# A two-block hybrid layer stack in split fp32: the feed-forwards' high weight parts get homes of their own, and the arena begins later

## The reference

```python
# first block
x = x + mix @ w_out                                   # mix: causal pools and an RWKV-7 scan
h2 = rms_norm(x, mlp_norm)
x = x + square(relu(h2 @ w_ffn_up)) @ w_ffn_down      # 2048 -> 8192 -> 2048
gate = sigmoid(rms_norm(x, ple_norm) @ w_ple_gate)    # 2048 -> 2048
x = x + gate * (p @ w_ple_proj)
x = rms_norm(x, final_norm)
# second block
h = x + concat([gla_out, nsa_out]) @ w_out_2          # gated linear attention, sparse attention
m = rms_norm(h, ffn_norm_g_2)
return h + (silu(m @ w_gate_2) * (m @ w_up_2)) @ w_down_2   # 2048 -> 5632 -> 2048
```

## Time and profile before

| | us |
|---|---|
| median of 3 runs | 2490.66 |
| lowest and highest | 2487.08, 2492.56 |
| the profiled execution's own time | 2493.05 |
| its span, first to last instruction | 2491.2 |
| mean granted TensorE clock | 0.993 |

### The profile page before, as it was taken

How to read it: one execution, slowest core, us unless ns; L and a number is a source line. 1 busy time by engine, 2 the same in 40 slices (tenths; PEclk the granted TensorE clock), 3 DMA queues, 4 the chain that set the end, 5 groups by cost and what they waited for, 6 DMA issues and landing times.

```text
span 2491.2 us, 40493 instructions
## 1 busy us (share of the span) xinstructions
PE 2458.7 (99%) x18716; PEld 2246.8 (90%) x18716; DVE 1361.0 (55%) x1130; ACT 989.0 (40%) x936; POOL 191.0 (8%) x139
## 2 busy tenths in 40 slices
PE   8999999999999999999999999999999999999999
PEld 7999988998998988988789999767998998999897
DVE  5597675444444444445457577565554554554543
ACT  4642244433333333344453363355433333333332
POOL 0003110120110110120000002000000000000000
PEclk9999999999999999999999999899999999999999
DMA  7552146555655656564555554234555664654643
GB/s 220 163 159 80 31 180 214 174 199 180 192 185 187 193 179 201 171 232 173 186 163 181 173 170 139 94 109 136 183 173 174 215 197 157 221 175 171 213 151 135
DMA packets 334533, 425.44 MB, mean 171 GB/s; under 512 B 4185, under 2 KB 249357, under 8 KB 333981
## 3 DMA queue, kind: packets, MB, share of 16 engines
q1 hardware_dynamic: 333053, 418.55, 51.4%
q0 software_dynamic: 1136, 4.17, 0.5%
q10 hardware_dynamic: 176, 0.14, 0.0%
HBM read 420.75 MB, written 2.10 MB: 170 GB/s over the span
## 4 chain that ended last, share of the span: by engine, by line
PE 91%; DVE 5%; issue 2%; ACT 1%; DMA 0%; POOLq 0%; POOL 0%; DVEq 0%; ACTq 0%
PE PS L596 81%; PE PS L795 2%; PE PS L686 1%; DVE ring_r L1900 1%; PE PS L632 1%; PE PS L969 1%; DVE ring_r L2170 1%; PE PS L1153 0%; PE PS L1249 0%; ACT arena_r L1323 0%; PE PS L853 0%; PE PS L908 0%; PE PS L1077 0%; DMA arena<-in_attn_norm 0%; PE PS L900 0%
## 5 line engine op out<-in xcount | busy, mean ns | idle before, releaser
L596 PE MATMUL PS<-arena_r,arena_r 128*128 128x256 f32 (+1 forms) x6976 | 1592.1, 304 | 3.9 <-DVE ring_r L2170 1.7
L596 PEld LDWEIGHTS PS<-arena_r,arena_r 128*128 128x128 f32 x6976 | 1142.3, 188 | 68.2 <-issue 5.5
L1858 DVE TENSOR_TENSOR ring_r<-ring,arena_r 128x2048 fp32r<-128x2048 f32 x316 | 730.7, 2316 | 686.9 <-ACT arena_r L1323 686.9
L1323 ACT ACTIVATE arena_r<-ring 128x2048 fp32r<-128x2048 f32 (+1 forms) x394 | 690.5, 1758 | 1005.6 <-PE PS L596 999.4
L596 PE MATMUL PS<-arena_r,ring_r 128*128 128x256 f32 x3072 | 861.4, 280 | 0.0
L596 PEld LDWEIGHTS PS<-arena_r,ring_r 128*128 128x128 f32 x3072 | 577.9, 188 | 0.0
L596 PE MATMUL PS<-ring_r,arena_r 128*128 128x512 f32 (+1 forms) x1504 | 544.0, 375 | 0.0
L596 PE MATMUL PS<-arena_r,actT_r 128*128 128x512 f32 (+1 forms) x1184 | 458.0, 387 | 0.0
L596 PEld LDWEIGHTS PS<-ring_r,arena_r 128*128 128x128 f32 x1504 | 276.4, 188 | 53.3 <-issue 1.4
L596 PEld LDWEIGHTS PS<-arena_r,actT_r 128*128 128x128 f32 x1184 | 223.3, 189 | 46.3
L596 PE MATMUL PS<-actT_r,arena_r 128*128 128x256 f32 (+1 forms) x656 | 185.2, 282 | 0.0
(11 more groups left out here) (334 smaller groups left out, 1429.0 us busy)
## 6 DMA issues: line engine op xcount, KB each, us to landing
ring<-in_w_ffn_up SPq DMA_DIRECT2D x32, 2048.0 KB, 9.3
ring<-in_w_ffn_down SPq DMA_DIRECT2D x32, 2048.0 KB, 8.1
ring<-in_w_in SPq DMA_DIRECT2D x22, 2048.0 KB, 8.2
ring<-in_w_gate SPq DMA_DIRECT2D x22, 2048.0 KB, 8.2
ring<-in_w_up SPq DMA_DIRECT2D x22, 2048.0 KB, 8.1
ring<-in_w_in SPq DMA_DIRECT2D x32, 1024.0 KB, 5.5
ring<-in_w_out SPq DMA_DIRECT2D x16, 2048.0 KB, 8.0
ring<-in_w_down SPq DMA_DIRECT2D x12, 2048.0 KB, 7.9
```

The costliest lines, as they stand in the source:

```text
L596: mm = pe.matmul(dst, r32(w, early), r32(x, early), start=first and q == 0, stop=last and q == 2)
L1323: return act.activation(dst, src, ACT.Copy, scale=scale)
L1858: v.tensor_tensor(r32(u), u, high_of(HIW[j]), ALU.subtract).then_inc(S["w_low"], counts(units, j))
```

## The change

`small` grows from 104 to 132 words (416 to 528 bytes), and nothing uses the new words; the arena behind it begins later. The high homes of the feed-forwards and of the gate no longer are the four common ones. They stand at word 16448 + 2112 j + 16 part, where part is the part of the feed-forward (0 to 3) and is 0 for the gate. All other stages keep the old homes. Since an old home of unit `j` overlaps the new homes of units `j` and `j + 1`, ScalarE waits for one unit more before it copies a unit of the first GLA group (`N_GLA`).

```diff
-    small = sbuf("small", [P, 104])
+    small = sbuf("small", [P, 132])
...
-    R32_AT = [(HIW_AT + 2048 * j, 2048) for j in range(4)] + [(at, KT * T) for at in (XH_AT, HTH_AT, HTL_AT)]
+    WIDE_AT = 16448
+    R32_AT = [(WIDE_AT, 8640)] + [(at, KT * T) for at in (XH_AT, HTH_AT, HTL_AT)]
...
-    HIW = [area(HIW_AT + 2048 * j, 2048) for j in range(4)]
+    def high_home(n, i, j):
+
+        if N_F1 <= n < N_GATE:
+            part = ((i or 0) + (n - N_F1) // 8) % F1_PARTS
+        elif n >= N_F2:
+            part = (i or 0) + (n - N_F2) // F2_N
+        elif N_GATE <= n < N_GLA:
+            part = 0
+        else:
+            return area(HIW_AT + 2048 * j, 2048)
+        return area(WIDE_AT + 2112 * j + 16 * part, 2048)
...
                 if not free:
-                    act.wait_ge(S["w_used"], used(n - 1, i, per, j + 1))
-                copy(r32(HIW[j]), unit_at(n % 2, j)).then_inc(S["w_high"], counts(units, j))
+                    act.wait_ge(S["w_used"], used(n - 1, i, per, min(j + 2, 4) if n == N_GLA else j + 1))
+                copy(r32(high_home(n, i, j)), unit_at(n % 2, j)).then_inc(S["w_high"], counts(units, j))
```

More of the change, by code:

```diff
@@ L607, in split_rows @@
                     pe.wait_ge(S["x_low"], XSPLIT[fresh] + 4 + 2 * j)
-                wh, wl = (a.rearrange("p (k n) -> p k n", k=8) for a in (HIW[j], unit_at(n % 2, j)))
+                wh, wl = (a.rearrange("p (k n) -> p k n", k=8) for a in (high_home(n, i, j), unit_at(n % 2, j)))
                 for f in range(2):
@@ L641, in split_tokens @@
                     ready(q)
-                wh, wl = (a.rearrange("p (k n) -> p k n", k=4) for a in (HIW[j], unit_at(n % 2, j)))
+                wh, wl = (a.rearrange("p (k n) -> p k n", k=4) for a in (high_home(n, i, j), unit_at(n % 2, j)))
                 for k in range(4):
@@ L1857, in low @@
                 u = unit_at(n % 2, j)
-                v.tensor_tensor(r32(u), u, high_of(HIW[j]), ALU.subtract).then_inc(S["w_low"], counts(units, j))
+                v.tensor_tensor(r32(u), u, high_of(high_home(n, i, j)), ALU.subtract).then_inc(S["w_low"], counts(units, j))
         def add_out(w, g, at, by=None):
```

## The result

The changed kernel is slower by a third of a per cent: ratio 1.0037, 95% interval 1.0026 to 1.0049, medians 2498.61 us against 2490.48 (7 runs each). Its profiled execution took 2498.06 us, with a span of 2496.3 against 2491.2. The time lies inside the stated range, 5.8 us above the forecast of 2492.8. By the prediction's own bound of 5 us the outcome is slower (+8.1 us), which had a chance of 0.27, and not the likeliest case, no clear change.

The account below looks back on a forecast made before the run. The prediction took TensorE's pitch of back-to-back matmuls to bound the kernel. Distances 0.0 and the wait +2.1 us gave 2495.2 us against the profiled run, 2492.8 us on the median, with a range of 2480 to 2504.

Parts of the forecast that it names:

- the prediction's own bound of 5 us: Whole kernel: a change under 0.2%, 5 us, is about what a measurement cannot tell from none.
- the likeliest case: Whole kernel: same time within 5 us, chance 0.53; the likeliest case alone is 2489 to 2497 us.
- The bound: Feed-forwards: TensorE has no idle time, so time is number of matmuls times pitch; other engines count only where TensorE waits.
- The wait at the first GLA group: End of gate: unit 2's copy goes ahead of the sigmoid, delaying VectorE, transposes and token copies; +2.1 us, from 1.2 to 2.9.
- The distances: Feed-forwards: operand distances modulo 128 set the pitch; parts 1 and 3 exchange two values, the gate keeps its own; 0.0 us.
- if bits above 128 bytes decide: Operand addresses: one stated sign of being wrong, as only low bits, modulo 128, were taken to matter; no size given.
- The term by stage: Feed-forwards: first ups -1.2, second ups +1.5, first downs -0.7, second downs +0.4 us, gate unchanged.
- half of either lottery: Ups: half settle one pitch step lower, 2483.5 us, or half of the second feed-forward's at 360 ns, 2499.8 us.
- The slower one: Second feed-forward's ups: half at 360 ns gives +9.1 us, 2499.8; all, 2506.7; decides from 2.9 us; chance 0.25.
- the bounds: Every stage at its outermost pitch steps: ups -18.6 to +13.9 us, downs and gate -3.1 to +10.1 us.
- faster twin: Ups of both feed-forwards settle one step lower: half gives -7.2 us, 2483.5; all, 2474; chance 0.22.
- No effect of distance: All matmuls: independent read ports make operand distance irrelevant, leaving only the wait, +2.1 us, 2492.8 us; chance 0.10.

Follow-up runs that it names:

- experiment 6: Changed kernel with the gate on its old homes, so the longer wait stands before the gate's copies; ratio 1.0031 to the kernel before.
- experiment 1: Kernel before with only the longer wait for the copies of the first GLA group; ratio 1.0009.
- experiment 2: Kernel before with only `small` 28 words longer, so the arena begins 128 bytes later; ratio 0.9999.
- experiment 3: Kernel before with an unused 32-word tensor ahead of all others, every operand 128 bytes later, distances between operands kept; ratio 0.9997.
- e7: Changed kernel with every new home 8 words (32 bytes) further; one run, 2504.33 us.
- e10: Kernel before with `small` at 112 words, so the arena begins 32 bytes later, old homes kept; ratio 1.0003.

## Why the prediction was right, and where it failed

**The bound.** Right: TensorE's pitch, with nothing else late in the feed-forwards. Same instructions, same shares of the page, and stage lengths that follow from pitch times triples.

**The wait at the first GLA group, +2.1 us.** Right, in every step of the chain. TensorE stands 1.07 us before the transposes (1.2 forecast) and again before the second unit, the token copies come 1.36 us behind the transposes' start instead of 0.64, and the stage is 1.9 us shorter once the wait stands elsewhere (experiment 6), 1.5 us longer with the wait alone (experiment 1).

**The distances, 0.0 us.** The step that failed is "so I take only the low bits to matter", where low meant modulo 128: by it, moving the arena by 128 bytes was to change nothing. The prediction named this as a sign of being wrong ("if bits above 128 bytes decide"), and it came. The later arena alone (experiment 2) moved the first ups from 355.6 to 353.3, the first downs from 690 to 686.7, and the second downs from 686.7 to 695, though all relations modulo 128 stayed. So parts 0 and 2, which were to keep their values, did not. Part by part, the second ups came as forecast (353.3, 355.6, 353.3, 355.6 against 353.4, 355.6, 353.3, 355.0), the first ups in the last part alone, the downs in no part. The term by stage, forecast against the stage lengths of the two traces: first ups -1.2, measured -2.2; first downs -0.7, measured +2.3; second ups +1.5, measured +1.2; second downs +0.4, measured +3.3. Gate 0, measured -0.6, and the output projection of the first block, which the forecast left out, -0.4. Together 0.0 against +3.6. That the time still fell inside the range is owed to a range drawn wide enough for half of either lottery, and not to this term.

**The rivals.** The slower one came, with the wrong place: it was put in the second ups (measured +1.2), and the price lay in the downs of both feed-forwards (+5.6), which stood only in the bounds, with the gate, as up to +10.1. It decided as written: with the wait's 2 us, 2.9 us of pitch are enough. Its faster twin is there too: part 2's ups fell to 346.7. No effect of distance is refuted by experiments 2 and 3 taken together. The Trainium skill (SBUF — State Buffer, the two separate sides) has TensorE's two read ports independent and TensorE waiting on no one; the same matmuls take 683 to 710 ns a triple here, by where the operands stand and how a stage is entered.

**What stays open.** The profiled pair differs by 5.0 us, the medians by 8.1. The profiled execution before was 2.6 us above its median. Part of such spread is TensorE's clock, in the second block's mixers. Experiment 3, whose feed-forwards are equal to those of the kernel before to 0.03 us, had a span of 2487.8 us and reached the second feed-forward 3.4 us sooner. 1.6 of them come from one stretch, here in the kernel before and then, at the same time of its span, in experiment 3 (length, busy TensorE, its loads, VectorE, ScalarE and GpSimd, granted clock, DMA share, GB/s):

```profile
1526.00:1529.40 3.40, 3.40 (x19) 3.40 (x17) 0.04 (x1) 0.22 (x1) 0.00 (x0) 0.50 0.01 2
```

```profile
1526.00:1529.40 3.40, 3.40 (x32) 3.40 (x31) 1.06 (x1) 1.06 (x1) 0.00 (x0) 1.00 0.00 0
```

In the first the granted clock is 0.50, the lower of its two levels (1.2 GHz), and triples take 640 ns; in the second it is 1.00, with triples of some 347. TensorE's work ahead of it was the same, 79 matmuls in the 10 us ahead of the same products. The changed kernel's trace has 0.50 there as well, for 6.8 us. The timed runs of the kernel before fit this: over the 82 that were measured beside the experiments, 31 with a mean granted clock of 0.993 average 2491.0 us and 23 with 0.995 average 2486.8. Inside the feed-forwards the clock is 1.00 in both traces, so the pitches above owe nothing to it. Whether the clock also makes up the 3 us between 5.0 and 8.1 is not shown. Nor is it shown what the operands collide in: the runs show that distance modulo 256 chooses the step, and that the same distances settle on more than one, most likely by the entry, but not the mechanism behind a step.

## What to carry to other kernels

Where a tuned kernel is bound by back-to-back matmuls, read the pitch per stage from starts and counts before believing that equal shapes cost the same, and compare it when a change moves buffers, even by a few unused words: here 28 of them took 2.3 us off the first ups and put 2.7 us on the second downs. Homes can be chosen for each kind of group from a sweep that gives every part a different distance, and the gain must then be measured in place, since the same addresses were seen on two steps, the likely reason being the entry. And when a wait is lengthened on an engine that works strictly in its order, follow what stands behind it: two of the three copies that wait longer cost nothing, and the third held up a sigmoid, two vector operations and TensorE's transposes.

## What the runs showed of the hardware

The pitch of a triple of fp32r matmuls at granted clock 1.00 stands in most stages on multiples of 6.67 ns: 346.7, 353.3 and 360.0 with 256 columns, 686.7, 693.3 and 700.0 with 512. Values between (355.6, 683.1, 690, 695, 696.7, and e7's 363.4) are means of a pattern of two to six triples that repeats: in the first feed-forward's downs of the kernel before, triples of 687 and 693 ns took turns, in those of e10 triples of 679 and 688. There a single triple need not stand on a step, but the pattern does: 679 + 688 is 205 times 6.67. A stage keeps its pitch over hundreds of triples, with ScalarE and VectorE busy or idle, and repeats it in another kernel with the same distances to 0.01 us of a stage of 90 us. For a matmul alone the Trainium skill (TensorE: Matmul & The Clock Gate, back-to-back issue gap) gives columns at 2.4 GHz and 2.5 ns more, an estimate of 327.5 and 647.5 ns for a triple; no feed-forward stage here came below 346.6 and 683.1. In these stages each matmul also has a load of the stationary operand of its own; no run here takes the loads away, so what they add is not shown.
